# The activations' operand tiles start 416 bytes, in place of 448, past a multiple of 512 from the split weights

## What is computed

```
x = x + 0.5 * swiglu(rmsnorm(x), ffn_w_in, ffn_w_out)     # 4 times, 1024 -> 2 x 2816 -> 1024
x = x + hgrn2_mixer(rmsnorm(x), a_w_in, ..., a_w_out)      # 1024 -> 4096, a chunked scan, -> 1024
x = x + mla_mixer(rmsnorm(x), k, v, w_dq, w_uq, w_out)     # 16 heads
x = x + sigmoid(rmsnorm(x) @ ple_w_gate) * (p @ ple_w_in)  # 2 times
...                                                        # then 2 layers of:
y = hybrid_mixer(rmsnorm(x) * (1 + scale) + shift, w_in, w_out)   # 1024 -> 3864 -> attention -> 1024
x = x + gate * rmsnorm(y)
```

## Time and profile before

| | us |
|---|---|
| median of 3 runs | 1559.37 (1559.15 to 1560.65) |
| the profiled execution's own time | 1557.95 |
| its span, first to last instruction | 1556.1 |
| TensorE busy in it | 1491.3 |
| VectorE busy | 1095.1 |
| ScalarE busy | 766.3 |
| mean granted TensorE clock | 0.979 |

### The profile page before, as it was taken

The page is one execution under the profiler, slowest core; times in us unless marked ns, Lnnn a source line. Parts: engine busy times, 40 slices in busy tenths (PEclk is TensorE's granted clock), DMA queues, the critical chain, the costliest instruction groups (busy, mean ns, idle before and its releaser), DMA issues.

```text
span 1556.1 us, 31034 instructions
## 1 busy us (share of the span) xinstructions
PE 1491.3 (96%) x12371; PEld 1436.0 (92%) x12371; DVE 1095.1 (70%) x1566; ACT 766.3 (49%) x1149; POOL 189.7 (12%) x227
## 2 busy tenths in 40 slices
PE   6999998999999999999999999999996999989998
PEld 6999998999999998999999899999996996879867
DVE  5886568986896677876677755887568557395683
ACT  5554355465554356444454454544354436354472
POOL 1111013711331010101010001110012000010000
PEclk9999999999999999999999999999997998999999
DMA  7787743345787646766646135776653751066400
GB/s 226 230 271 231 246 147 124 90 128 162 236 271 229 211 136 191 246 219 215 217 129 177 55 122 173 233 251 218 223 160 108 208 149 55 1 181 186 125 1 28
DMA packets 219308, 264.86 MB, mean 170 GB/s; under 512 B 22253, under 2 KB 197325, under 8 KB 219213
## 3 DMA queue, kind: packets, MB, share of 16 engines
q1 hardware_dynamic: 209136, 234.58, 48.5%
q0 software_dynamic: 8960, 27.37, 5.3%
q10 hardware_dynamic: 1117, 1.57, 0.3%
HBM read 262.44 MB, written 1.05 MB: 169 GB/s over the span
## 4 chain that ended last, share of the span: by engine, by line
PE 81%; DVE 12%; ACT 4%; DMA 2%; issue 1%; POOL 0%; SPq 0%; DVEq 0%; ACTq 0%
PE twin L1081 24%; PE twin L1082 24%; PE twin L1083 24%; DVE w_lo L1774 3%; DMA w_raw<-in_ffn_w_in 1%; PE twin L1488 1%; PE twin L1700 1%; ACT w_hi L700 1%; DVE rs L1803 1%; DVE hg_s L1992 1%; PE twin L1502 1%; PE twin L1500 1%; PE twin L1662 1%; DVE hg_f L1974 1%; DVE sq L1973 1%
## 5 line engine op out<-in xcount | busy, mean ns | idle before, releaser
L700 ACT ACTIVATE w_hi<-w_raw 128x1024 fp32r<-128x1024 f32 (+1 forms) x452 | 453.6, 1038 | 459.3 <-PE twin L1083 279.9
L1081 PE MATMUL twin<-xh,w_lo 128*128 128x256 f32 x2312 | 653.5, 283 | 26.2 <-DVE xl L2260 15.0
L1774 DVE TENSOR_TENSOR w_lo<-w_raw,w_hi 128x1024 fp32r<-128x1024 f32 (+1 forms) x452 | 548.1, 1249 | 166.0 <-ACT w_hi L700 165.6
L1082 PE MATMUL twin<-xl,w_hi 128*128 128x256 f32 x2312 | 648.4, 280 | 0.0
L1083 PE MATMUL twin<-xh,w_hi 128*128 128x256 f32 x2312 | 648.2, 280 | 0.0
L1081 PEld LDWEIGHTS twin<-xh,w_lo 128*128 128x128 f32 x2312 | 440.3, 190 | 31.4 <-DVE xl L2260 16.1
L1082 PEld LDWEIGHTS twin<-xl,w_hi 128*128 128x128 f32 x2312 | 439.6, 190 | 1.5 <-issue 1.2
L1083 PEld LDWEIGHTS twin<-xh,w_hi 128*128 128x128 f32 x2312 | 438.1, 189 | 0.2
L1081 PE MATMUL twin<-hh,w_lo 128*128 (+1 forms) x704 | 195.6, 278 | 0.0
L1082 PE MATMUL twin<-hl,w_hi 128*128 (+1 forms) x704 | 195.2, 277 | 0.0
L1083 PE MATMUL twin<-hh,w_hi 128*128 (+1 forms) x704 | 195.2, 277 | 0.0
(11 more groups left out here) (363 smaller groups left out, 2077.4 us busy)
## 6 DMA issues: line engine op xcount, KB each, us to landing
w_raw<-in_ffn_w_in SPq DMA_DIRECT2D x176, 512.0 KB, 4.7
w_raw<-in_ffn_w_out SPq DMA_DIRECT2D x88, 512.0 KB, 4.2
w_raw<-in_w_in SPq DMA_DIRECT2D x52, 512.0 KB, 4.7
mod_raw<-in_w_ada POOLq DMA_DIRECT2D x128, 192.0 KB, 4.4
w_raw<-in_a_w_in SPq DMA_DIRECT2D x32, 512.0 KB, 4.2
w_raw<-in_ple_w_gate SPq DMA_DIRECT2D x16, 512.0 KB, 4.2
w_raw<-in_b_w_out SPq DMA_DIRECT2D x16, 512.0 KB, 3.7
w_raw<-in_w_out SPq DMA_DIRECT2D x16, 512.0 KB, 4.5
```

What stands on the lines that cost most here:

```text
L700: A(w_hi[:, c % NSLOT, cols], w_raw[:, c % NRAW, cols], ACT.Copy).then_inc(*did(hi_ready))
L1081: mm(out, lhs[1], rhs[0], start=start, stop=False, skip_group_check=skip)
L1082: mm(out, lhs[0], rhs[1], start=False, stop=False, skip_group_check=skip)
L1774: V.tensor_tensor(w_lo[:, c % NSLOT, cols], w_raw[:, c % NRAW, cols], f32(w_hi[:, c % NSLOT, cols]), ALU.subtract).then_inc(*did(lo_ready))
```

## The change

```diff
-OPERAND_STEP = 448
+OPERAND_STEP = 416
```

## The result

| | before | after |
|---|---|---|
| median of the runs, us | 1559.26 (1551.06 to 1560.65, 4 runs) | 1579.59 (1576.52 to 1583.54, 4 runs) |
| profiled execution, us | 1557.95 | 1578.58 |
| span, us | 1556.1 | 1576.8 |
| TensorE busy, us | 1491.3 | 1515.6 |
| span less TensorE busy, us | 64.8 | 61.2 |

The change makes the kernel slower: the ratio is 1.0174, 95% interval 1.0138 to 1.0210. The medians of the table are only 20 us (1.3%) apart, while a ratio of 1.0174 means 27 us. I had forecast 13. The sign is right and the time lies in the range, but the size is that of rival B, in which no quick stretch is left. The fourth run of before took 1551.06 us, 8 us less than the three that I had seen; the experiments come back to that.

What follows compares the result with a forecast made beforehand. TensorE at one of two paces was taken to bound the kernel. On the profiled execution 1557.95 + 13 + 0 + 0 = 1571 us, or 1572.4 us on the medians; range 1541 to 1590 us.

Steps and rivals of the forecast that it cites:

- rival B: TensorE's three-pass matmuls: no quick stretch is left; +26 us to 1585 us, or 1596 us at 118.8 ns; chance 0.17.
- quick stretch: Window in which TensorE's three-pass matmuls run at 113.3 ns, not the tardy 117.8 ns; 503.5 us of windows before.
- What bounds the kernel: TensorE's own pace sets the time, with slightly over half of its three-pass matmuls at the quicker of two paces.
- Step 1: All queues: no instruction added, removed or reordered, so no queue changes and no wait is added.
- Step 2, the distance: TensorE's three-pass matmuls: operand distance 448 to 416 loses half of the quick stretches, +13 us.
- the floor: TensorE's three-pass matmuls: 113.3 ns is what the moving operand needs alone, without the full weight load in its way.
- Step 3, the start at 32 modulo 64: ScalarE and VectorE accesses to moved tiles: 0 taken, bound -1 to +2 us.
- Step 4, the landings: DMAs landing in moved tiles, chiefly 128 loads of mod_raw: 0 taken, bound +1 us.
- A: TensorE's three-pass matmuls: the tardy pattern vanishes, up to 21 us given back, put at 1543 us; chance 0.24.
- D: TensorE: the change does nothing, all stretches keep their pace; 1559.4 +/- 1 us; chance 0.08.
- C: TensorE's product loops: distance is not the cause, any change deals the stretches anew; 1553 to 1566 us; chance 0.21.

Runs made afterwards that it cites:

- the second experiment's kernel: Against before: distance 416 by moving w_hi and w_lo up 32 bytes, every other tile at its old address modulo 512; 1579.79 us, ratio 1.0158.
- the 39: 39 more runs of the unchanged kernel, in three same-chip comparisons with the experiments; 1546.72 to 1564.33 us, median 1554.1 us.
- the pair above: Profiled executions of before and of a kernel with weights and all tiles behind them 32 bytes higher, both at distance 448: 1557.95 and 1549.10 us.
- the first experiment: Against before: w_hi, w_lo and everything behind them start 32 bytes higher, distance kept at 448; 1549.81 us, ratio 0.9978.

## Why the prediction was right or wrong

*What bounds the kernel* held. All of the cost is TensorE's pace, and between the two profiled executions it came through to the end less 3.6 us of waits that it covered.

*Step 1* (no other instruction matters) held: 31034 instructions in both.

*Step 2, the distance.* The mechanism held: it is the distance between the operands. The size was wrong, and the failing step is the interpolation. I took 416 to lie halfway between "64 away from a multiple of 512, half the matmuls at the floor" and "128 away, none", and so took half of the quick stretches as lost, 26 / 2 = +13 us. The table shows that there is no such slope. Quick stretches exist at odd multiples of 64 and at no other distance that was tried; 32 bytes to either side, at 416 and 480, not one group is quick. The term should have been rival B's whole one, all quick stretches lost. B gave +26 us at a pace of 117.8 ns for all. TensorE's busy time measured +24.3 us, with a mixture of 117.3 and 118.7 ns, and 20.7 us were left at the end of these two executions. By the medians it is 24 us for the second experiment's kernel against its 19 runs of before, and 25 us for the changed kernel against the 39. I gave B 0.17, and the forecast 0.30.

That the forecast of 1572.4 us lies only 7 us below the measured 1579.6 is luck: its base of 1559.4 us was 5 us above the median of the 39 runs, and this hid part of a term that was 12 us too small.

The rows had a hint that I weighed wrongly. The two distances at which the trace shows 113.3 ns, 448 and its mirror 64, and the one at which it doesn't, 128, fit a class as well as a slope, and a set of paces with nothing in between speaks for a class.

*Step 3, the start at 32 modulo 64*, held at 0. VectorE's and ScalarE's groups on moved tiles, by their mean ns, first before and then after:

```profile
L1780 DVE SCALAR_TENSOR_TENSOR xl<-X,col,xh 128x256 fp32r<-128x256 f32 x72 | 30.4, 478 | 1.8 <-ACT xh L706 1.8
...
L748 ACT ACTIVATE hh<-hid_t 128x512 f32 x40 | 24.8, 620 | 13.7 <-DVE hid_t L1866 13.7
```

```profile
L1780 DVE SCALAR_TENSOR_TENSOR xl<-X,col,xh 128x256 fp32r<-128x256 f32 x72 | 30.4, 478 | 1.8 <-ACT xh L706 1.8
...
L748 ACT ACTIVATE hh<-hid_t 128x512 f32 x40 | 24.8, 620 | 11.9 <-DVE hid_t L1866 11.8
```

The kernel with everything shifted says the same from the other side. *Step 4, the landings*, held at 0 too: `mod_raw` lands in 4.4 us in both, and VectorE's wait for it went from 39.4 to 35.4 us:

```profile
L1823 DVE SCALAR_TENSOR_TENSOR mod_acc<-mod_raw,csf,mod_acc 128x384 f32<-128x384 f32 x112 | 65.1, 619 | 35.8 <-DMA mod_raw<-in_w_ada 35.4
```

*The floor.* That the weight load disturbs the moving reads was my reading of the mechanism, and no experiment took the load away. The 24-column chunk of the changed kernel bears on it: 21 intervals take 2.40 us, 114.3 ns, next to chunks of the same `xh` and `xl` at 118.7.

```profile
1297.80 0.28 PE L1083 MATMUL twin<-xh,w_hi 128*24 128x256 f32 x1
...
1300.20 0.28 PE L1083 MATMUL twin<-xh,w_hi 128*24 128x256 f32 x1
```

Its slices are 96 bytes apart, so its distances differ from matmul to matmul; all the same it stays near the floor. That supports the reading and doesn't prove it.

*The rivals.* A (the tardy pattern vanishes) is refuted: the old tardy pace of 117.8 is gone indeed, but replaced by 117.3, a gain of 0.4% there. D is refuted too: the distance alone moves the pace from 113.3 to 120.0 ns. The Trainium skill ("SBUF — State Buffer", section "Who interferes with whom") calls TensorE's two read ports independent; taken as a rule for the time, as in D, it does not hold here. Whether the two reads meet behind the ports or something else in TensorE depends on the addresses, no run tells. C (the stretches are dealt anew) is not the cause of the change, but it is real. My argument against it, that three runs lay within 1.5 us, was an accident of three: the next ones spread over 17 us. For the sum this means that the 1559 us of before was on the high side of its own spread (the 39 later runs have a median of 1554.1), that a few runs can't tell 3 us from no change, as I had assumed they could, and that a forecast from the quick share of one profiled execution carries up to some 10 us of luck with it (8.85 us in the pair above).

## What to carry to other kernels

When TensorE is the bound and loads new weights for every matmul, read its pace from the distance of starts, stretch by stretch; a group's mean hides a 4% step in two populations. The address of one operand relative to the other can decide which of them occur: try all multiples of 32 bytes within 256, not a neighbour or two, since the paces come in classes and a value between two known ones need not lie between them. And where a kernel's executions differ by 1%, look whether stretches of the same loop run at two paces, before three close runs are taken for its time.

## What the runs showed of the hardware that was not expected

For float32r matmuls of 128 weight columns and 256 moving columns at a granted clock of 1.00 (2.4 GHz), the distance of starts takes few values: 113.3, 117.3, 117.8, 118.7 and 120.0 ns, and 118.0 to 118.6 at distance 480. Which of them occur depends on the distance between the operands' addresses. Modulo 256, as far as was tried, 64 and 192 allow 113.3 and 117.8 ns, 160 gives 117.3 and 118.7 and at times 120.0, 128 gives 118.5 to 118.7 and now and then 120.0, 224 gives 118.3, and 0 gives 120.0. With the operands' roles exchanged, 480 gives 116.8 ns and 416 gives 120.0; that the sign of the distance turns with the roles fits this, since `ckh` and `ckl` at 96, the negative of 416, run at 119.4 to 120.2 in the usual roles, but it is shown by nothing more. Where two paces are allowed, one can hold for 100 us and more, through breaks of 0.2 us. At 64 and 320 the quick one is rare in the usual roles (13% of the groups). At 448 and 192 it has half of them in the executions of the table and, at 448, over four fifths in that of the first experiment, although the two paces themselves are the same. Why is not known from these runs.
